# Two-row moving operand for gate streams and output projections in a two-block transformer kernel

## The reference, cut to what matters

```python
def hybrid_mixer(h, w_in, ...):
    q, f_logit, i_in, g_out, b_gate, c_gate, u, gate_a, gate_b = split_projection(h, w_in)
    ...
    o = rms_norm(hgrn2_chunk_recurrence(qh, k, heads(i_in), log_f), g_norm_w) * jax.nn.silu(heads(g_out))
    y_a = o @ w_proj_hgrn
    v = b_gate * u                       # then a causal convolution of 3 taps: conv
    y_b = (c_gate * conv) @ w_proj_conv
    merged = jax.nn.sigmoid(gate_a) * y_a + jax.nn.sigmoid(gate_b) * y_b
    return merged @ w_out
def hyena_mixer(...):      ...; return z @ w_out + b_out
def window_attention(...): ...; return o @ w_o
x = x + mixer(rmsnorm(x))
```

## Time and profile before

| | |
|---|---|
| median of 3 runs | 2823.06 us (2822.19 to 2823.51) |
| the profiled execution | 2827.12 us, span 2825.3 us |
| mean granted TensorE clock | 0.993 of full |
| TensorE busy | 2768.1 us, 98% |
| VectorE busy | 2103.0 us, 74% |
| ScalarE busy | 1639.1 us, 58% |
| GpSimd busy | 487.7 us, 17% |
| chain that ended last | TensorE 90%, VectorE 7% |

### The profile page before, as it was taken

The page is one execution under the profiler, slowest core; times in us unless marked ns, Lnnn a source line. Parts: engine busy times, 40 slices in busy tenths (PEclk is TensorE's granted clock), DMA queues, the critical chain, the costliest instruction groups (busy, mean ns, idle before and its releaser), DMA issues.

```text
span 2825.3 us, 41185 instructions
## 1 busy us (share of the span) xinstructions
PE 2768.1 (98%) x17248; PEld 2460.9 (87%) x17248; DVE 2103.0 (74%) x1969; ACT 1639.1 (58%) x1662; POOL 487.7 (17%) x311
## 2 busy tenths in 40 slices
PE   8999999999999999999999899999999999999999
PEld 8999988999988888888888778888898888877888
DVE  6866776686769889888899789665666566589664
ACT  5546554554657777777777654554655465454552
POOL 1220331123010000000000023231023123123330
PEclk9999999999999999999999999999999999999999
DMA  7444565645449899899899922555445555732563
GB/s 231 159 156 163 182 190 182 190 154 163 156 151 370 341 366 372 331 368 376 333 368 365 346 75 90 166 189 191 172 143 186 180 171 185 226 115 92 164 190 123
DMA packets 359711, 612.40 MB, mean 217 GB/s; under 512 B 11519, under 2 KB 323925, under 8 KB 324832
## 3 DMA queue, kind: packets, MB, share of 16 engines
q1 hardware_dynamic: 355936, 597.99, 60.8%
q10 hardware_dynamic: 3104, 11.58, 1.2%
q0 software_dynamic: 480, 0.12, 0.0%
HBM read 608.47 MB, written 1.05 MB: 216 GB/s over the span
## 4 chain that ended last, share of the span: by engine, by line
PE 90%; DVE 7%; DMA 1%; ACT 1%; issue 1%; SPq 0%; DVEq 0%; ACTq 0%
PE ps L377 22%; PE ps L378 11%; PE ps L364 8%; PE ps L366 8%; PE ps L365 8%; PE ps L1409 5%; PE ps L1411 5%; PE ps L1410 5%; PE ps L1387 3%; PE ps L1385 3%; PE ps L1386 3%; DVE wlo L291 2%; PE ps L776 1%; PE ps L1964 1%; PE ps L1976 1%
## 5 line engine op out<-in xcount | busy, mean ns | idle before, releaser
L291 DVE TENSOR_TENSOR wlo<-raw,whi 128x2048 fp32r<-128x2048 f32 (+2 forms) x574 | 1323.7, 2312 | 320.2 <-ACT whi L280 301.4
L280 ACT ACTIVATE whi<-raw 128x2048 fp32r<-128x2048 f32 (+2 forms) x574 | 1085.7, 1893 | 239.0 <-PE ps L378 112.7
L377 PE MATMUL ps<-HXB,whi 128*128 128x512 f32 x1760 | 618.3, 397 | 2.7 <-DVE HXB L512 2.7
L364 PE MATMUL ps<-HX,whi 128*128 128x256 f32 x1680 | 485.6, 289 | 17.2 <-DVE wlo L291 13.4
L378 PE MATMUL ps<-HXB,wlo 128*128 128x256 f32 x1760 | 490.3, 279 | 0.0
L365 PE MATMUL ps<-HX,whi 128*128 128x256 f32 x1680 | 476.4, 284 | 0.0
L366 PE MATMUL ps<-HX,wlo 128*128 128x256 f32 x1680 | 476.4, 284 | 0.0
L377 PEld LDWEIGHTS ps<-HXB,whi 128*128 128x128 f32 x1760 | 330.9, 188 | 82.8 <-DVE HXB L512 3.9
L364 PEld LDWEIGHTS ps<-HX,whi 128*128 128x128 f32 x1680 | 323.5, 193 | 23.3 <-ACT HX L587 11.6
L378 PEld LDWEIGHTS ps<-HXB,wlo 128*128 128x128 f32 x1760 | 331.8, 189 | 0.2
L365 PEld LDWEIGHTS ps<-HX,whi 128*128 128x128 f32 x1680 | 323.6, 193 | 3.4 <-issue 3.3
(11 more groups left out here) (345 smaller groups left out, 4048.6 us busy)
## 6 DMA issues: line engine op xcount, KB each, us to landing
raw<-in_c_experts SPq DMA_DIRECT2D x264, 1024.0 KB, 4.9
raw<-in_w_in SPq DMA_DIRECT2D x71, 1024.0 KB, 5.0
raw<-in_ff_w_gate SPq DMA_DIRECT2D x44, 1024.0 KB, 5.3
raw<-in_ff_w_up SPq DMA_DIRECT2D x44, 1024.0 KB, 5.3
raw<-in_ff_w_down SPq DMA_DIRECT2D x32, 1024.0 KB, 5.1
raw<-in_dense_w SPq DMA_DIRECT2D x30, 1024.0 KB, 5.2
raw<-in_hy_w_in SPq DMA_DIRECT2D x24, 1024.0 KB, 5.2
raw<-in_ff_w_down SPq DMA_DIRECT2D x16, 768.0 KB, 4.3
```

The costliest lines, as they stand in the source:

```text
L280: e.activation(m.whi[:, i % NSPLIT, 0:n], m.raw[:, i % NRAW, 0:n], ACT.Copy).then_inc(*k.up("act", "hi", i))
L291: e.tensor_tensor(m.wlo[:, i % NRAW, 0:n], m.raw[:, i % NRAW, 0:n], hi, ALU.subtract).then_inc(*k.up("dve", "lo", i))
L364: e.matmul(o, wh, xh, start=first and t == k0, stop=False)
L377: e.matmul(o[:, :], wh, x[:, :, kx + t, :], start=first and t == k0, stop=False)
```

## The change

b, c, ga, go and out of the recurrent layers, out of both Hyena layers and out of attention now use the wide form. For the gates ScalarE copies the low half of the pair to SBUF, and VectorE adds the high half on top, in place; the pair is free after that. For out VectorE adds both halves to the residual one after the other.

```diff
--- before.py
+++ after.py
@@ -404,6 +404,15 @@
 
 
 
+
+
+def pe_wide_gemms(e, k, m, s, name, x, cols, fresh=None, after=None):
+
+    for j in cols:
+        pe_wide_gemm(e, k, m, s, name, x, j, fresh=fresh)
+        fresh = None
+        if after:
+            after(j)
 
 
 def pe_sums(e, k, m, s, c0, n):
@@ -632,6 +641,7 @@
 STEPS = (("b", 0), ("b", 1), ("u", 0), ("u", 1), ("c", 0), ("c", 1), ("ga", 0), ("ga", 1), ("go", 0), ("go", 1))
 
 
+GATES = {"b": 5, "c": 6, "ga": 10, "go": 3}
 PLACE = {1: 10, 2: 3, 3: 8, 4: 9, ACROSS: 3}
 READ_BEFORE = {3: 0, 4: 0, ACROSS: 2}
 
@@ -711,7 +721,10 @@
         mm.then_inc(*k.up("mm", "v", s, h))
         k.note("mm", "used", i)
     for i, (name, half) in enumerate(STEPS):
-        pe_gemm(e, k, m, s, name, m.HX, range(2 * half, 2 * half + 2))
+        if name == "u":
+            pe_gemm(e, k, m, s, name, m.HX, range(2 * half, 2 * half + 2))
+        else:
+            pe_wide_gemms(e, k, m, s, name, m.HX, range(2 * half, 2 * half + 2))
         if i < ACROSS:
             pe_scores(e, k, m, s, i)
         if i == ACROSS:
@@ -751,7 +764,7 @@
     pe_gemm(e, k, m, s, "proj", m.OX, range(4), fresh=("ox", s))
     if l == 1:
         pe_hold(e, k, m, "route", s)
-    pe_gemm(e, k, m, s, "out", m.HX, range(4), fresh=("mx", s), after=lambda j: pe_route(e, k, m, s, 2 * j - 2) if l and j else None)
+    pe_wide_gemms(e, k, m, s, "out", m.HX, range(4), fresh=("mx", s), after=lambda j: pe_route(e, k, m, s, 2 * j - 2) if l and j else None)
 
 
 def pe_route(e, k, m, s, c0):
@@ -780,8 +793,9 @@
 def act_hgrn(e, k, m, panels, s, last, l, nxt):
     def evac(name, j, dst):
         e.wait_ge(*k.at("g", s, name, j))
-        e.activation(m.buf(dst)[:, j * 512:j * 512 + 512], ps(k, m, "g", s, name, j)[:, :], ACT.Copy).then_inc(
-            *k.up("act", "free", "g", s, name, j))
+        low = pair_halves(k, m, "g", s, name, j)[1]
+        e.activation(m.buf(dst)[:, j * 512:j * 512 + 512].rearrange("p (a n) -> p a n", a=2), low, ACT.Copy).then_inc(
+            *k.up("act", "low", s, name, j))
 
     def conv_high(cs):
         for c in cs:
@@ -841,7 +855,7 @@
         for j in (2 * half, 2 * half + 1):
             act_panel(e, k, m, panels)
             if name in ("b", "c", "ga", "go"):
-                evac(name, j, {"b": 5, "c": 6, "ga": 10, "go": 3}[name])
+                evac(name, j, GATES[name])
             if name == "go" and j:
                 curve("go", j - 1, 3, ACT.Silu, "normed", s, "go", j - 1)
         if i >= 7:
@@ -962,6 +976,11 @@
                 e.tensor_tensor(vp[:, 2 * j:2 * j + 2, 2:], m.buf8(5)[:, 2 * j:2 * j + 2, :],
                                 ps(k, m, "g", s, "u", j)[:, :].rearrange("p (a n) -> p a n", a=2), ALU.mult).then_inc(
                     *k.up("dve", "free", "g", s, "u", j))
+            else:
+                e.wait_ge(*k.at("low", s, name, j))
+                x = m.buf(GATES[name])[:, j * 512:j * 512 + 512].rearrange("p (a n) -> p a n", a=2)
+                e.tensor_tensor(x, x, pair_halves(k, m, "g", s, name, j)[0], ALU.add).then_inc(
+                    *k.up("dve", "free", "g", s, name, j))
         if i >= 8:
             dve_conv(e, k, m, s, l, (2 * i - 16, 2 * i - 15))
         if i == 9:
@@ -1048,8 +1067,10 @@
 def dve_add_x(e, k, m, s, name, j):
     e.wait_ge(*k.at("g", s, name, j))
     x = m.X[:, 2 * j:2 * j + 2, :]
-    e.tensor_tensor(x, x, ps(k, m, "g", s, name, j)[:, :].rearrange("p (a n) -> p a n", a=2), ALU.add).then_inc(
-        *k.up("dve", "free", "g", s, name, j))
+    high, low = pair_halves(k, m, "g", s, name, j)
+    e.tensor_tensor(x, x, high, ALU.add).then_inc(*k.up("dve"))
+    e.wait_ge(*k.own("dve"))
+    e.tensor_tensor(x, x, low, ALU.add).then_inc(*k.up("dve", "free", "g", s, name, j))
     k.note("dve", "x", s, 2 * j)
     k.note("dve", "x", s, 2 * j + 1)
 
@@ -2061,7 +2082,7 @@
     for j in range(12):
         pe_gemm(e, k, m, s, "in", m.HX, [j], fresh=None if j else ("hx", last))
         pe_between(e, k, m, s, j)
-    pe_gemm(e, k, m, s, "out", m.OX, range(4), fresh=("zx", s))
+    pe_wide_gemms(e, k, m, s, "out", m.OX, range(4), fresh=("zx", s))
 
 
 def act_absolute(e, k, m, s, o_):
@@ -2351,11 +2372,15 @@
     dve_result(e, k, m, s, range(4, 8))
     for j in range(4):
         e.wait_ge(*k.at("g", s, "out", j))
-        o = ps(k, m, "g", s, "out", j)
+        high, low = pair_halves(k, m, "g", s, "out", j)
         for i in range(2):
             ch = 2 * j + i
-            e.scalar_tensor_tensor(m.X[:, ch, :], o[:, i * L:(i + 1) * L], m.col("hy_b_out_2", 8 * f + ch), m.X[:, ch, :],
-                                   ALU.add, ALU.add).then_inc(*k.up("dve", "x", s, ch))
+            e.scalar_tensor_tensor(m.X[:, ch, :], high[:, i, :], m.col("hy_b_out_2", 8 * f + ch), m.X[:, ch, :],
+                                   ALU.add, ALU.add).then_inc(*k.up("dve"))
+        e.wait_ge(*k.own("dve"))
+        both = m.X[:, 2 * j:2 * j + 2, :]
+        e.tensor_tensor(both, both, low, ALU.add).then_inc(*k.up("dve", "x", s, 2 * j))
+        k.note("dve", "x", s, 2 * j + 1)
         k.note("dve", "free", "g", s, "out", j)
         if j:
             dve_ahead(e, k, m, s, 2 * j - 2, 2, nxt)
@@ -2562,7 +2587,7 @@
     values(3)
     for g in (1, 2, 3):
         back(g)
-    pe_gemm(e, k, m, s, "out", m.HX, range(4), fresh=("ax", s))
+    pe_wide_gemms(e, k, m, s, "out", m.HX, range(4), fresh=("ax", s))
 
 
 def act_attn(e, k, m, a, panels, s, last, nxt):
```

## The result

| | before | after |
|---|---|---|
| median, 20 executions each in turn | 2822.69 us | 2828.76 us |
| ratio after to before | | 1.0021 [1.0014, 1.0028] |
| the profiled execution | 2827.12 us | 2829.26 us, span 2827.4 us |

The change costs 6 us. The forecast was 2819.5 us in a range of 2813 to 2826, with 0.09 for slower by over 0.2%. One of the kernel before's 20 executions, at 14,766 us, stands alone and does not move the median.

The account below looks back on a forecast made before the run. TensorE, busy for 98% of the span, was taken as the bound. Panels -9.9, ends of out +3.6 and level steps +2.8 gave -3.5 us, so 2819.5 us from a median of 2823.06, range 2813 to 2826.

Parts of the forecast that it names:

- slower by over 0.2%: Outcome for the whole kernel: measured time rises by more than a measurement tells from no change, about 5.6 us; chance 0.09.
- 52 panels: TensorE's changed gate and out panels gain 0.20 us each, less 0.5 us swallowed: -9.9 us.
- five ends of out: After each out's last panel a second, dependent VectorE add delays the residual by 0.72 us, five times: +3.6 us.
- level steps, two layers: In the recurrent layers' b and c steps TensorE waits for VectorE's new adds: 1.4 us lost per layer, +2.8 us.
- the bounds: Gain per panel from narrow to wide: between 0.105 us (slow wide stretch) and 0.211 us (fast one).
- the 0.4 below which the forecast called itself wrong: Sign: a pair of c, ga or go panels should shrink by 0.4 us, or the forecast is wrong.
- Banks: A wide pair holds two of eight banks until VectorE has added; waits for them were to cost nothing.
- ScalarE's copies: Copies from the gate panels become two rows of 256 instead of one of 512, at the same cost.
- the terms are the same for that one: The profiled execution's -3.5 us was applied unchanged to the median of 2823.06 us, giving 2819.5 us.
- "slower" rival: VectorE bounds the level steps through collisions with GpSimd, 13 us in two layers: +6.7 us, 2830 us; chance 0.08.

Follow-up runs that it names:

- e6: Kernel before, all panels narrow, with one more dependent VectorE operation behind each residual add: 2823.95 against 2822.27 us, 1.0009.
- e5: Kernel before, unchanged, against itself and profiled once more: ratio 1.0006.
- e13: Kernel before with five more pairs of harmless transposes in the second recurrent layer: 2829.53 against 2819.09 us, 1.0045.
- e1: Changed kernel, unedited, measured and profiled again against the kernel before: 2826.73 against 2820.19 us, 1.0022.
- e11: Changed kernel with five more pairs of harmless transposes in the first recurrent layer, against the kernel before: 2819.38 us, 1.0000.
- e12: Changed kernel with ten more pairs of harmless transposes in the first recurrent layer, against the kernel before: 2819.63 us, 0.9995.
- e14: Changed kernel with five more pairs of harmless transposes in the second recurrent layer, against the kernel before: 2823.55 us, 1.0014.
- e8: Changed kernel with b and the last panel of each out narrow, against the kernel before: 2814.55 us, 0.9972; a second series 0.9986.

## Why the prediction was wrong

**The terms that the forecast has.**

| term | forecast | measured from the stages |
|---|---|---|
| 52 panels | -9.9 | -7.2: ga and go 16 x 0.105, b 8 x 0.105, c 8 x 0.2 (a pair 11.18 for 11.59), out 3.0 in all |
| five ends of out | +3.6 | +3.5 (0.66 to 0.73 each) |
| level steps, two layers | +2.8 | +1.7 |
| sum | -3.5 | -2.0 |

- *Panels.* "I take 0.20, since the 0.35 us of single k-tiles goes with the faster stretch" was mis-sized for b, ga and go. A k-tile of 0.347 and one of 0.354 both read as 0.35, so single starts could not choose between the bounds. b, ga and go got 0.105, the other end; c got 0.2 and attention's out (23.11 - 22.27) / 4 = 0.21, as forecast. A pair of ga or go panels shrank by 0.21 us, not by the 0.4 below which the forecast called itself wrong.
- *End of out.* Right, in place and size. The fifth k-tile is 0.65 us late (forecast 0.7), the link is 0.72 us, and e6 has it alone.
- *Level steps.* Right in mechanism. GpSimd's first multiplications start at 98.67 (forecast 98.7), 5.3 us later than before, and the second group 2.5 us later (3 to 5 were forecast), the scores of level 2 at 128.79 (factors forecast for 129.1), ACROSS at 173.49 (173.7). TensorE waits 1.9 us in layer 1 and 0.6 in layer 2, for 1 to 2 in each, and in layer 1 at level 1 as well, where no wait was forecast. But the loss against before is smaller, since the earlier trace rows came from an execution that hid a wait of the kernel before. Its granted clock near the start, and that of the same kernel in e5:

```profile
19.00:24.00 5.00, 3.18 (x14) 2.76 (x14) 4.96 (x5) 3.97 (x4) 1.96 (x2) 0.75 1.10 327
```

```profile
19.00:24.00 5.00, 3.89 (x32) 3.51 (x30) 5.00 (x3) 3.97 (x4) 1.97 (x2) 1.00 1.12 326
```

  With the clock full TensorE arrives at the steps 1.25 us earlier and waits there for the same VectorE; e5's chain goes through the factors at level 2, where that of before has TensorE alone (e6 and e13, narrow too, have e5's longer steps):

```profile
126.54 1.14 DVE work L1076
127.73 3.84 PE ps L776 x32
```

- *Banks, and ScalarE's copies:* no cost, as said. VectorE did not become the bound of the steps, and ga and go show no wait.

**The step that failed.** It is the sum itself, "-9.9 + 3.6 + 2.8 = -3.5 us", with "the terms are the same for that one" behind it: it has terms only for the stages that the diff touches and takes the rest as unchanged. The touched stages did give -2.0 us. The measured +6 is the rest, which no rival had: the "slower" rival is VectorE at the levels, and it did not happen (its 13 us are 1.7). In its place stand two stages that the diff does not touch: the sums behind the experts, 3.2 to 4.3 us longer, where TensorE waits for its own instructions, and pooling, 2.5 to 4.4 us longer than in e5, where it waits for a load and gets more of the lower clock.

The balance closes only in part. The first profile of the change is 7.0 us longer than e5's (spans of 2827.4 and 2820.4): +3.9 in the sums, +4.4 in pooling, +2.6 in attention, where the lower clock came in this execution and not in the second, and the touched stages at -3.4 with the clock that each had. e1 is 2.6 us longer than e5: +4.3, +2.5, and the touched stages at -4.9, since e5 had the lower clock in both Hyena outs and e1 had it in neither; smaller differences make up the rest. That -2.0 and +4.3 come near those 2.6 us is luck. Over the executions of e1 the mean granted clock is 0.9928 and the kernel before's 0.9942, 3.8 us of 2820, part of it in these same stages. Which stretches get it differs between executions, of which only one in a series has a trace. e11 and e12 speak against the loss being the change's own work: with ten or twenty matmuls more it is level with the kernel before. e14, with ten more in layer 2, is still 0.14% slower.

**Is the change worth anything?** With its instructions placed well in the sums, nothing that can be told in e11 and e12 (1.0000 and 0.9995), and a small loss in e14 (1.0014). The version of e8 is shorter in its own stages by some 5 us (c at the faster rate, ga and go at the slower one, out without the late residual), and measured 0.9972 and 0.9986, but with ten or twenty matmuls more 0.9996 and 1.0003. It beats the kernel before as it stands, by an amount that moves as much with placement as with its merit.

## What to carry to other kernels

When a kernel is at 98% of one engine, sum the touched stages, but compare all stages between two profiles before believing either the sum or the measurement, and go on behind the first one that differs (here pooling differed too). Take two profiles of the same kernel first: one execution hid a wait of 1.2 us here. A difference of 0.2 to 0.4% can come from where the program's instructions fall; add a handful of harmless ones to both kernels before calling such a difference the change's, and where TensorE stands with "issue", look at when the blocks of the instruction queue land. Read a rate from a long stretch, never from one step that is rounded to 10 ns.

## What the runs showed of the hardware

- The same two matmuls of a wide k-tile run steadily at 0.347 or at 0.354 us (44.46 and 45.30 us for eight panels), both at full granted clock. A whole feed-forward layer can have the one rate or the other in two executions of one program, 3.4 us apart.
- TensorE's instructions come in blocks of 16 KB, and behind the branch the next block is late: TensorE resumed 1.2 to 1.6 us after it landed, in nine of twenty profiles, and lost 0.35 to 3.9 us by where among sixteen like matmuls the boundary lay.
- Ten matmuls more, over 1,000 us ahead, went with 0.28 to 0.45% more time in three series, and twenty with none. The boundary then lay behind the third of the sixteen matmuls in all three profiles, with 3.4 to 3.9 us of "issue".
- GpSimd delays VectorE's operations with two SBUF inputs by some 1.1 us a piece: L668 took 3.40 us and, with GpSimd later, 2.28. It leaves those that read PSUM alone: the four predicated copies beside it took 2.61 us before, 0.65 each. This is the rule of the Trainium skill, "SBUF — State Buffer", section "SBUF: two separate sides", and the rows agree; here it gave the adds part of their price back.
